# A decoder trunk on one core: unit places, V row places and repeated products of the second half

## What is computed

```python
# 1. h += W_o( sig(g_a) * W_a(StickBreakingAttn(q,k,v)) + sig(g_c) * W_c(B * conv3(C * xc)) )
#    where [q,k,v,xc,B,C,g_a,g_c] = RMSNorm(h) @ W_in
# 2. h += CrossAttn(RMSNorm(h), RMSNorm(mem))      (4 heads, 256 memory tokens)
# 3. h += PEER(RMSNorm(h))                         (8 retrieval heads, 128^2 single-neuron experts)
q = (xn @ w_query).reshape(b, s, 8, 2, 128)
sc = jnp.einsum('bshcd,hcnd->bshcn', q, sub_keys)
top_s, top_i = lax.top_k(sc, 16)
cand_s = top_s[..., 0, :, None] + top_s[..., 1, None, :]        # 16 x 16 sums
cand_i = top_i[..., 0, :, None] * 128 + top_i[..., 1, None, :]
best_s, best_pos = lax.top_k(cand_s, 16)                         # 16 experts a head: 128 a token
gates = jax.nn.softmax(best_s, axis=-1)
u = expert_u[ib]                                                 # a row of 1024 for each expert chosen
act = jax.nn.gelu(jnp.einsum('ced,cd->ce', u, xb))
out = jnp.einsum('ce,ced->cd', gb * act, expert_v[ib])
```

## Time and profile before

| | us |
|---|---|
| median of 3 runs | 2021.76 |
| lowest and highest of them | 2018.59, 2022.65 |
| the profiled execution | 2023.32 |
| its span, from first to last instruction | 2021.6 |
| PE busy in it | 1925.9 (95%) |
| DVE busy in it | 1166.8 (58%) |

### The profile page before, as it was taken

How to read it: one execution, slowest core, us unless ns; L and a number is a source line. 1 busy time by engine, 2 the same in 40 slices (tenths; PEclk the granted TensorE clock), 3 DMA queues, 4 the chain that set the end, 5 groups by cost and what they waited for, 6 DMA issues and landing times.

```text
span 2021.6 us, 23901 instructions
## 1 busy us (share of the span) xinstructions
PE 1925.9 (95%) x9007; PEld 1244.1 (62%) x9007; DVE 1166.8 (58%) x2908; ACT 446.2 (22%) x1045; POOL 871.3 (43%) x786
## 2 busy tenths in 40 slices
PE   8999999999989999999998889999999989999998
PEld 7688886856866888885766766444445543333332
DVE  1022111002968888788889999877768764533321
ACT  2233211121202454221211354000013321111112
POOL 0000000000756433545657455645557776656643
PEclk9999999999989999999999678999999989999999
DMA  7533454433999977999899687999999999999997
GB/s 245 151 115 113 146 157 147 146 104 125 365 333 390 315 257 245 365 385 384 325 361 380 227 275 246 403 409 409 409 385 369 368 376 410 409 409 409 409 370 291
DMA packets 252440, 613.48 MB, mean 303 GB/s; under 512 B 18677, under 2 KB 121125, under 8 KB 252325
## 3 DMA queue, kind: packets, MB, share of 16 engines
q0 software_dynamic: 110592, 402.70, 52.7%
q1 hardware_dynamic: 141120, 208.17, 29.8%
q10 hardware_dynamic: 612, 1.07, 0.2%
HBM read 609.77 MB, written 2.10 MB: 303 GB/s over the span
## 4 chain that ended last, share of the span: by engine, by line
PE 68%; DMA 15%; DVE 9%; POOL 4%; issue 2%; ACT 1%; SPq 0%; ACTq 0%; DVEq 0%; POOLq 0%
PE ps L620 27%; PE ps L899 11%; PE ps L849 9%; DMA u_rows<-in_peer_u_dram,idx 8%; PE ps L635 7%; DVE u_rows L1398 4%; PE ps L889 3%; PE ps L662 3%; DMA v_rows<-in_peer_v_dram,idx_turned 3%; DMA wring<-in_w_in_dram 2%; POOL u_rows L579 2%; POOL v_rows L593 2%; DMA wring<-in_peer_w_query_dram 1%; PE ps L649 1%; PE ps L688 1%
## 5 line engine op out<-in xcount | busy, mean ns | idle before, releaser
L579 POOL DMA_INDIRECT u_rows<-in_peer_u_dram,idx x512 | 589.1, 1151 | 971.7 <-DVE idx L1384 505.0
L1398 DVE CUSTOM_DVE_ANT_0 u_rows<-u_rows,xn 128x1024 f32<-128x1024 f32 x512 | 621.0, 1217 | 171.1 <-DMA u_rows<-in_peer_u_dram,idx 167.8
L620 PE MATMUL ps<-xT,wring 128*128 128x256 f32 x2432 | 553.0, 386 | 25.5 <-DMA wring<-in_peer_w_query_dram 11.7
L620 PEld LDWEIGHTS ps<-xT,wring 128*128 128x128 f32 x2432 | 462.8, 193 | 94.5 <-DMA wring<-in_peer_w_query_dram 13.3
L899 PE MATMUL ps<-d_rows,gates 128*128 128x512 f32 x1024 | 456.3, 599 | 0.0
L899 PEld LDWEIGHTS ps<-d_rows,gates 128*128 128x128 f32 x1024 | 190.2, 190 | 266.0 <-issue 265.2
L849 PE MATMUL ps<-v_rows,diag 64*64 64x512 f32 x1928 | 247.0, 631 | 18.1 <-DMA v_rows<-in_peer_v_dram,idx_turned 18.1
L593 POOL DMA_INDIRECT v_rows<-in_peer_v_dram,idx x121 | 131.9, 1090 | 115.1 <-PE ps L849 92.7
L889 PEld LDWEIGHTS ps<-hot_b,hot_a 128*128 128x128 f32 x1024 | 142.7, 224 | 50.5 <-issue 33.5
L1094 ACT ACTIVATE diag<-ident,wgt 128x64 f32<-128x64 f32 x256 | 76.1, 336 | 426.4 <-PE ps L849 415.8
L889 PE MATMUL ps<-hot_b,hot_a 128*128 128x64 f32 x1024 | 150.1, 311 | 15.8 <-DVE hot_b L1465 11.1
(11 more groups left out here) (202 smaller groups left out, 1713.5 us busy)
## 6 DMA issues: line engine op xcount, KB each, us to landing
wring<-in_w_in_dram SPq DMA_DIRECT2D x128, 512.0 KB, 5.0
d_rows<-in_peer_v_dram SPq DMA_DIRECT2D x128, 512.0 KB, 6.8
wring<-in_peer_w_query_dram SPq DMA_DIRECT2D x32, 512.0 KB, 9.0
wring<-in_w_branch_conv_dram SPq DMA_DIRECT2D x16, 512.0 KB, 4.5
wring<-in_w_branch_attn_dram SPq DMA_DIRECT2D x16, 512.0 KB, 5.3
wring<-in_w_out_dram SPq DMA_DIRECT2D x16, 512.0 KB, 4.7
wring<-in_xattn_wq_dram SPq DMA_DIRECT2D x16, 512.0 KB, 4.8
wring<-in_xattn_wo_dram SPq DMA_DIRECT2D x16, 512.0 KB, 5.6
```

The source lines that it names most:

```text
L579: pool.indirect_dma_start(out=u_rows[:, n % URING, :], out_offset=None, in_=peer_u[0], in_offset=bass.IndirectOffsetOnAxis(ap=experts_of(g ...
L620: mm = pe.matmul(bank(job)[:, 0:HN], w[:, k % 4, P * b:P * (b + 1)], act[:, k, :], start=(k == 0), stop=(k == KT - 1))
L1398: dve.tensor_tensor_reduce(out=u, in0=u, in1=(xn2 if h else xn1)[:, i, :], scale=1.0, scalar=0.0, op0=ALU.mult, op1=ALU.add, accum_out=dot ...
```

## The change

It has four parts, all in the second half.

1. `PLACES`: the units from step 84 on stand later, by 1 step at first, 5 at the end of attention, 6 to 8 from step 118 on; the last two go from 250 and 254 to 255.
2. `CH_SLOT` of the first 32 chunks is spread over 36 steps, not 34: the last one stands in step 302, not 300. Blocks 64 to 127 stand two steps earlier (433 to 512).
3. `V_SLOT`: 28 rows instead of 14 stand in steps 302 to 405. The 84 rows of the second set of chunks stand in 406 to 433 (407 to 432 before), and behind step 433 there are 122 rows instead of 136, 38 of them from step 512 on (26 before). Row 128 moves from step 440 to 432.
4. `table_transposes`: the 4 repeated products ahead are gone, and 12 in the middle become 4. Also, on DVE in `select` (line 1338) the sum of one value with 8 others is a `tensor_tensor` in place of a `tensor_scalar`, 32 times in all.

```diff
-    CH_SLOT = spread(12, 46, 32) + spread(151, 177, 32)
+    CH_SLOT = spread(12, 48, 32) + spread(151, 177, 32)
...
-    BLK_SLOT = spread(48, 149, 64) + spread(179, 260, 64)
-    V_SLOT = (spread(24, 46, 22) + spread(48, 150, 14) + spread(151, 177, 84) + spread(179, 256, 110)
-              + spread(256, 280, 26))
+    BLK_SLOT = spread(48, 149, 64) + spread(177, 258, 64)
+    V_SLOT = (spread(24, 46, 22) + spread(46, 80, 9) + spread(80, 115, 18) + spread(115, 150, 1) + spread(150, 178, 84) + spread(178, 210, 36) + spread(210, 240, 27) + spread(240, 256, 21) + spread(256, 268, 21) + spread(268, 280, 17))
...
-              218, 220, 224, 228, 233, 237, 242, 246, 250, 254]
+              223, 225, 225, 227, 231, 235, 240, 244, 249, 253, 255, 255]
...
                 pe.wait_ge(x3_done, 2 * HT)
-                keep_running(4)
                 for b in range(NJB):
...
                 mm.then_inc(t_done, 1)
-                keep_running(12)
+                keep_running(4)
                 pe.wait_ge(wgt_rdy, HG)
...
-                t0 = after(dve.tensor_scalar(rest_of_first, top_v[:, 1, near:TOPK], top_v[:, 0, 0:1], None, ALU.add))
+                t0 = after(dve.tensor_tensor(rest_of_first, top_v[:, 1, near:TOPK],
+                                             top_v[:, 0, 0:1].to_broadcast([P, near]), ALU.add))
```

## The result

| | before | after |
|---|---|---|
| median of 22 runs each, us | 2024.59 | 2032.13 |
| lowest and highest, us | 2016.89, 2032.19 | 2024.76, 2040.49 |
| the profiled execution, us | 2023.32 | 2024.76 |

The changed kernel takes 1.0038 times as long, 95% interval 1.0027 to 1.0049: 7.7 us slower. The forecast was 2016.8 us, and its range ended at 2027.

A forecast was written before the change was run, and what follows sets the result against it. PE was taken to bound the second half's front and everything after 1257 us, DVE the first 32 gate chunks. Terms of -2.7, +3.3, -1.9, -3.0 and -0.7 sum to -5.0: 2016.8 us against the 2021.8 median, range 2008 to 2027.

The forecast's parts named there:

- Units later: Second half's front from step 80: DVE, 7 steps ahead, gives them back at step 261; 0 us, bounds -10.0 and +2.
- Four products, not sixteen: At the weights' table behind the front: fewer repeated PE products ready it sooner, ending DVE's wait at step 268; -2.7 us.
- Two steps more: First 32 gate chunks: DVE does two more U steps before the last chunk, at 1.66 us each; +3.3 us.
- 14 rows more before step 406: Blocks 0 to 63: V rows still come late, but one more pair fills PE's wait behind block 63; -1.9 us.
- the second rival: Steps 336 to 371: V rows come too late for PE, at most 9.7 us, 2026.5 us in all; chance 0.15.
- Second set of chunks and block 64: Before block 64: PE's wait for a row and a slow pair go, a new wait for additions comes; -3.0 us.
- The last stretch: From block 0: fewer runs of pairs, -0.7 us; behind the last block 18 pairs instead of 11, 0, +5 at most.
- The faster front: In 1036 to 1110 us PE's front ends earlier, its 10.0 us idle gone; 2006.8 us, at half price 2011.8; chance 0.20.
- The clock's mechanism: From step 280, over 22 steps: PE stays at 1.2 GHz; up to +33 us, a part gives 2027; chance 0.06.
- the four for "right": Step 261 wait some 10 us; block 0 within 1.5 of 1257; block 63/64 waits 4 or less; no PE idle behind.
- those for "wrong": Front ends before 1105; V-row waits over 3 us; clock 0.5 beyond 1200 us; wait for additions over 5 us.
- The sum: Whole kernel: -2.7 + 3.3 - 1.9 - 3.0 - 0.7 = -5.0, so 2016.8 us against the median; chance 0.45.

The follow-up runs named there:

- the half rows: The kernel before and places_only, each with the U rows of steps 116 to 199 gathered at half width; ratios to before 0.9977 and 0.9987.
- slots_only: The kernel before with parts 2 and 3 of the change alone (chunks, blocks and V rows by the new tables); ratio 0.9997.
- all_parts: The whole change run once more, against the kernel before; ratio 1.0027.
- rest_later: The kernel before with only the units behind attention moved, 6 to 8 steps later; ratio 1.0076.
- places_only: The kernel before with part 1 of the change alone (the later units); ratio 1.0038.

## Why the prediction was wrong, point by point

- **Units later: 0, with bounds -10 and +2.** This is the first step that failed. What it says of DVE at step 261 holds: 0.95 us early became 10.46. But it priced only what DVE gains at the end, and covered the way there with "DVE has 55.5 us of idle time". Idle time of DVE is not idle time of the DMA engines, and the same has them at 0.92 of their time and 328 GB/s there. Seven U rows are 3.7 MB, or 9 us of all engines at 409 GB/s, brought forward into a stretch in which weights of 512 KB are wanted on time. Measured: +7.7 us for the part (3.2 to 11.9). The stretches account for 5.3 of it: +3.4 in attention in the mean, from a wait for DVE of 2.80 instead of 1.58 us and the half clock behind it; the forecast had that mechanism in its "+2". Behind attention +5.3 up to the unit that waits for `xattn_wq`, from the weights, as the half rows show, and -3.4 again to the front's end.
- **Four products, not sixteen: -2.7.** Right: -3.0 to -3.1 in the stretch, -4.2 in the time (-0.2 to -8.5). PE's pause and the lower clock that it brings cost nothing.
- **Two steps more: +3.3.** +3.3 in after and +3.2 in `slots_only`, but +1.4 in `all_parts` and +1.1 to +1.3 in four more: the right sign, and 2 us too high in five of seven profiles.
- **14 rows more before step 406: -1.9.** The stretch of the blocks became 15.5 us longer against the 14.6 of the sum. The waits behind block 63 stayed (4.40 us against 3.94), so the gain of 1.9 does not show there. PE is not idle at all in blocks 0 to 63 of after (251.90 of 251.90 us): the second rival is out.
- **Second set of chunks and block 64: -3.0.** The stretch from block 63 to block 64 is 10.8 us shorter in after than in before, and 7.9 in the means (156.4 us in eight profiles with the new order, 164.3 in ten with the old). One pair fewer is 1.9 of it, leaving -6.0 against the -4.9 of this step and the one ahead: right within 1.1 us.
- **The last stretch: 0, +5 at most.** This is the second step that failed, by its size and by its likeliest value. The right number was in it, 36 rows at 1.28 us = 46 us, and was set aside with "up to 16 are in place before". 16 rows had indeed been asked for when block 127 ended (20 issues followed), but not all of them had come: the gathers' queue still moved 12.20 MB in the 38.1 us, 23 rows of 0.524 MB, so some 13 of the 36 were in place (an estimate from these numbers), and 1.05 MB of the output went out in between. The DMA engines are full up to that point (394 GB/s in blocks 64 to 127). Measured: 38.1 us, 6.7 more than the 7 added pairs explain.
- **Rivals.** The faster front did not come: it ends later, in all three profiles, though its last stretch may be shorter, as said above. The slow one that I gave a chance had a full DMA queue as its mechanism but the wrong place, steps 336 to 371 instead of the front and the tail. The clock's mechanism exists, 5.8 us in two profiles, and neither of them has the edit that was to bring it.
- **The signs.** Of the four for "right" the first came. Block 0 starts at 1260.3, the waits behind block 63 and before block 64 are 5.1 us together, and PE is idle 5.7 us in the last pairs. Of those for "wrong", the clock at 0.5 beyond 1200 us was no sign at all, since before has it there too.
- **The sum** with the two failed steps set right is -5.0 + 7.7 + 6.7 = +9.4 us, or +7.0 with the 5.3 of the stretches for the units; measured are +7.7. That it comes out so near is partly luck, since the parts measured by themselves add up to only +2.8.

What stays open: 4 of the 7.7 us lie in no stretch of the two profiles. Why the half clock comes behind some waits is open too, and their length alone does not decide it: PE ran at half clock for some 7 us behind the wait of 2.31 us in the earlier trace rows, and at full clock behind the one of 2.83 us at the same place in after.

## What to carry to other kernels

When work is moved earlier, ask of each stretch it enters which resource is full there, and price the moved work's bytes at the full rate of the DMA engines as well as its instructions; an idle engine beside full queues is no room. Work with a gather behind it that is pushed to the end is paced by the same rate even when little else runs beside it: 1.28 us for each row of 512 KB against 0.87 us of TensorE's use. Where two causes have nearly the same pace, as the issue and the bytes of a row had here, halve one of them and leave the other, and look at what of the loss goes and what stays. Compare the same instructions over all profiles at hand: a loss of 5 us in the middle of a stretch was hidden by its end.

## What the runs showed of the hardware

- In `rest_later`, with gathers and plain loads both queued, the engines served as many packets of one as of the other (1264 and 1281 in 15 us), so the loads with 1 KB packets got 85 of 394 GB/s. A load of 512 KB took 23 to 24 us so, and 6 to 9 us where at most four rows were ahead. Whether larger packets would bring the weights sooner was not tried.
- GpSimd issues one gather of 128 rows per 1.24 us (0.94 and 0.30 between), the same at 4 KB and at 2 KB a row (1.25), just under the 1.28 us that the bytes of the larger take.
- The granted clock fell to half for 3.4 us behind a wait of TensorE of 2.75 to 2.80 us in attention, in all five kernels with that wait, and not behind one of 1.50 to 1.65 us in the other thirteen. It also did behind the waits of 3.02, 2.76 and 2.85 us for `xattn_wq` in after, `all_parts` and `places_only`, and behind 2.31 us in the earlier trace rows, but not behind 2.83 us in after.
- Between the first gate chunk and block 0, where VectorE sets the pace, 51 and 58 us in a row at half clock left the stretch at 130 us; with 65 us it was 135.6, and VectorE waited 6.5 us for TensorE in it.
- On VectorE, adding one value per partition to 8 others took 0.225 us as a `tensor_scalar` and 0.158 us as a `tensor_tensor` (median of 32 each, in before and after).
